# A decoder layer in split float32: GpSimd makes the low parts of the weights, and the bias table DMAs go by SyncE's queue

## Chip, cores and metric

One core of one Trainium2 chip runs the kernel in one launch. The metric is the time on the device in microseconds (us). The kernel before takes 1284.85 us, the median of three runs (1284.72 to 1285.17).

## What is computed

One layer of a hybrid decoder with 512 tokens and a model width of 1024, all float32: a half-step gated feed-forward block (width 2816), a mixer of two attention branches whose outputs are gated and summed, and a second half-step feed-forward block. The weights are read once from HBM.

```python
x = x + 0.5 * swiglu(rms_norm(x, ffn1_norm), ffn1_w_gate, ffn1_w_up, ffn1_w_down)
h = rms_norm(x, mix_norm)
c_q, c_kv, k_rope, q_d, k_d, v_d, g_a, g_b = split(h @ w_in)
y_a = causal_latent_attention(c_q, c_kv, k_rope; w_uq, w_ukv) @ w_br_mla      # 8 heads
y_b = dilated_attention(q_d, k_d, v_d; T5 bias of rel_bias) @ w_br_dil        # 3 groups of 8 heads
x = x + (sigmoid(g_a + b_a) * y_a + sigmoid(g_b + b_b) * y_b) @ w_out
x = x + 0.5 * swiglu(rms_norm(x, ffn2_norm), ffn2_w_gate, ffn2_w_up, ffn2_w_down)
y = rms_norm(x, norm_final)

def swiglu(h, w_gate, w_up, w_down):
    return (silu(h @ w_gate) * (h @ w_up)) @ w_down
```

## The kernel before

Activations lie transposed in SBUF, features on the 128 partitions and the 512 tokens along the row. A weight product is done in three matmuls for each 128x128 tile: a float32 operand is the sum of a high part, rounded to the fast format, and a low part, and TensorE computes high by high, high by low and low by high (`multiply`, lines 365 to 377; the up products have the same three in line 540).

All weights come as one stream of 222 pieces of up to eight tiles (128x1024, 512 KB), numbered through the whole kernel: `up1` 44, `down1` 24, `latent` 6, `mla` 16, `dil` 48, `merge` 8, `out` 8, `up2` 44, `down2` 24. The down products' pieces have 8, 7 and 7 tiles, the latent up-projections ("lora") 5, and two of every twelve dilated pieces 4. For each piece:

- SyncE issues its load into one of four raw buffers (`load`, line 345). It waits until the low part of the piece four back is made.
- ScalarE makes the high part `w_hi` in one of two split buffers (`split_hi`, line 351). It waits for the load and until the piece two back is multiplied.
- VectorE makes the low part `w_lo = raw - w_hi` (`split_lo`, line 359) and counts it in `lo_ready`.
- TensorE waits for `lo_ready` and multiplies, and counts the piece in `piece_done`.

Each engine's order is written out by hand, so every split stands at a fixed place between the other operations of ScalarE and VectorE. The places that matter here:

- Start: x comes in eight chunks, and pieces 0 to 3 among them (lines 412 to 424). Up product (`up_turn`): two pieces make a gate and an up chunk; VectorE scales the gate (L1255), ScalarE takes the silu, VectorE scales and multiplies (L1259, L1261), ScalarE rounds the hidden chunk (L914), VectorE makes its low part (L1266). Before the first piece 3, TensorE spreads the norm over the tokens (L507) behind its wait for the low part of piece 3.
- Second turn of the first up product: VectorE also computes the rotation angles (L1196 to L1223) and the rows of the T5 bias (`bias_rows`, L1229, `rows_ready`). GpSimd then stores 16 copies of these rows to HBM (`skew`, L470), and after the last lora product reads them back as bias tables with 24 DMAs (L480), since their SBUF is shared with the latents.
- Down product (`down_turn`): after the third part of a chunk VectorE adds to x (L1284), ScalarE rounds the new activation (L875) and squares it (L885), VectorE makes the activation's low part (L1170) and adds the square (L1182). The second part's high part stands behind these on ScalarE.
- Latent attention (`attention`): for a head, VectorE takes the maxima of the scores (L1445), ScalarE the exponentials (L1022), VectorE normalises (L1458); in between it takes the next head's key, value (L1437, L1438) and query (L1420 to L1433).
- Merge: VectorE multiplies gate and branch (L1683, L1687) and adds (L1691), ScalarE rounds (L1133), VectorE makes the low part (L1694). The next high part stands behind L1133. Output product: VectorE adds to x (L1703), then ScalarE and VectorE go on as in the down product.

Before the change GpSimd does only small DMAs and, at the very end, two multiplications of the output (L486).

## Time and profile before

| what | value |
|---|---|
| median of three runs | 1284.85 us |
| the profiled execution | 1285.54 us |
| its span, first to last instruction | 1283.7 us |
| granted TensorE clock, mean | 0.999 |
| chain that ended last, shares | TensorE 94%, VectorE 2%, DMA 1%, issue 1%, ScalarE 1% |
| HBM | 92 GB/s over the span, 118 MB |

The profile is one execution, so its time stands beside the median and not for it. Its times are microseconds from the span's start. Its engines are PE (TensorE's matmuls), PEld (its weight loads), DVE (VectorE), ACT (ScalarE), POOL (GpSimd) and SP (SyncE); L361 is line 361 of the kernel before. TensorE is at work all the time and heads the chain, so a time is best read by where two matmul starts lie further apart than usual, and by how long before a piece's first matmul its low part was there. Matmuls are pipelined, so a duration of 0.39 us says little; the distance of starts does.

### The profile page before, as it was taken

The numbers are of one execution on the slowest core, as the hardware profiler recorded it, in microseconds if no ns is written. First come the engines' busy times: TensorE is split into PE (matmuls) and PEld (weight loads), VectorE is DVE, ScalarE is ACT, GpSimd is POOL, SyncE is SP. The second block draws the span as 40 slices with busy tenths as digits, with TensorE's granted clock in tenths as the row PEclk, the third lists the DMA queues.
The fourth block names the chain that finished last, engine by engine and source line by source line (L and its number), as shares of the span: only waits on it lengthen the run. The fifth ranks groups of instructions, "written<-read, shape, count | busy, mean of one in ns | idle before, by whom it ended". The sixth has DMA issues, their size and how long they took to land.

```text
span 1283.7 us, 16607 instructions
## 1 busy us (share of the span) xinstructions
PE 1270.7 (99%) x5998; PEld 1031.0 (80%) x5998; DVE 669.6 (52%) x984; ACT 442.9 (35%) x763; POOL 18.8 (1%) x36
## 2 busy tenths in 40 slices
PE   9999999999999999999999999999999999999997
PEld 6788888888888777787878878788888888888886
DVE  5744444433336777575655747676644444443323
ACT  5333322322233445343343424423433322332221
POOL 0000000000000000300000000000000000000000
PEclk9999999999999999999999999999999999999999
DMA  6342223333322221522222121223222223233321
GB/s 213 99 112 98 98 98 98 90 91 94 102 92 71 64 69 66 131 67 82 81 73 93 65 92 56 83 97 99 99 98 98 98 98 98 95 86 96 93 89 65
DMA packets 36003, 118.38 MB, mean 92 GB/s; under 512 B 4680, under 2 KB 4680, under 8 KB 35968
## 3 DMA queue, kind: packets, MB, share of 16 engines
q1 hardware_dynamic: 34416, 114.83, 27.6%
q0 software_dynamic: 1264, 3.06, 1.4%
q8 instruction: 20, 0.33, 0.1%
q14 instruction: 15, 0.12, 0.0%
q10 hardware_dynamic: 288, 0.03, 0.0%
HBM read 115.36 MB, written 2.55 MB: 92 GB/s over the span
## 4 chain that ended last, share of the span: by engine, by line
PE 94%; DVE 2%; DMA 1%; issue 1%; ACT 1%; SPq 0%; DVEq 0%; ACTq 0%
PE bank L540 36%; PE bank L374 17%; PE bank L376 17%; PE bank L375 17%; PE bank L723 1%; PE bank L746 1%; PE bank L643 1%; PE bank L670 1%; DMA x<-in_x_t 1%; DVE mla_stats L1445 1%; PE bank L763 1%; PE bank L659 1%; PE bank L759 1%; ACT w_hi L356 0%; PE bank L732 0%
## 5 line engine op out<-in xcount | busy, mean ns | idle before, releaser
L361 DVE TENSOR_TENSOR w_lo<-raw,w_hi 128x1024 fp32r<-128x1024 f32 (+2 forms) x221 | 258.8, 1171 | 228.8 <-ACT w_hi L356 226.7
L356 ACT ACTIVATE w_hi<-raw 128x1024 fp32r<-128x1024 f32 (+2 forms) x221 | 224.3, 1015 | 429.7 <-PE bank L540 228.3
L540 PE MATMUL bank<-act_hi,w_hi 128*128 128x512 f32 x704 | 217.8, 391 | 1.6 <-DVE act_lo L1170 0.8
L540 PE MATMUL bank<-act_hi,w_lo 128*128 128x512 f32 x704 | 216.9, 389 | 0.0
L540 PE MATMUL bank<-act_lo,w_hi 128*128 128x512 f32 x704 | 216.8, 389 | 0.0
L374 PE MATMUL bank<-act_hi,w_hi 128*128 128x512 f32 x528 | 212.0, 401 | 2.0 <-DVE w_lo L361 1.2
L376 PE MATMUL bank<-act_hi,w_lo 128*128 128x512 f32 x528 | 206.2, 391 | 0.0
L375 PE MATMUL bank<-act_lo,w_hi 128*128 128x512 f32 x528 | 205.8, 390 | 0.0
L540 PEld LDWEIGHTS bank<-act_hi,w_hi 128*128 128x128 f32 x704 | 131.6, 188 | 31.7 <-DVE w_lo L361 2.6
L540 PEld LDWEIGHTS bank<-act_hi,w_lo 128*128 128x128 f32 x704 | 132.1, 188 | 27.7
L540 PEld LDWEIGHTS bank<-act_lo,w_hi 128*128 128x128 f32 x704 | 132.1, 188 | 27.4
L375 PE MATMUL bank<-hid_lo,w_hi 128*128 128x512 f32 x352 | 136.9, 389 | 0.0
L374 PE MATMUL bank<-hid_hi,w_hi 128*128 128x512 f32 x352 | 136.9, 389 | 0.0
L376 PE MATMUL bank<-hid_hi,w_lo 128*128 128x512 f32 x352 | 136.9, 389 | 0.0
L374 PEld LDWEIGHTS bank<-act_hi,w_hi 128*128 128x128 f32 x528 | 99.1, 188 | 27.2 <-issue 6.0
L376 PEld LDWEIGHTS bank<-act_hi,w_lo 128*128 128x128 f32 x528 | 99.1, 188 | 21.5
L375 PEld LDWEIGHTS bank<-act_lo,w_hi 128*128 128x128 f32 x528 | 99.3, 188 | 18.7
L1255 DVE TENSOR_TENSOR work<-bank,rstd 128x512 f32<-128x512 f32 x44 | 30.4, 691 | 122.9 <-PE bank L540 122.8
L374 PEld LDWEIGHTS bank<-hid_hi,w_hi 128*128 128x128 f32 x352 | 66.1, 188 | 13.8
L375 PEld LDWEIGHTS bank<-hid_lo,w_hi 128*128 128x128 f32 x352 | 66.1, 188 | 13.8
L376 PEld LDWEIGHTS bank<-hid_hi,w_lo 128*128 128x128 f32 x352 | 66.1, 188 | 13.5
L914 ACT ACTIVATE hid_hi<-work 128x512 f32 (+1 forms) x44 | 27.8, 632 | 94.4 <-DVE work L1261 94.4
(177 smaller groups left out, 1052.5 us busy)
## 6 DMA issues: line engine op xcount, KB each, us to landing
raw<-in_ffn_up SPq DMA_DIRECT2D x87, 512.0 KB, 3.3
raw<-in_w_dil SPq DMA_DIRECT2D x40, 512.0 KB, 3.3
raw<-in_ffn_down SPq DMA_DIRECT2D x32, 448.0 KB, 3.3
raw<-in_ffn_down SPq DMA_DIRECT2D x16, 512.0 KB, 3.5
raw<-in_w_mla_gates SPq DMA_DIRECT2D x8, 512.0 KB, 3.3
raw<-in_w_branches SPq DMA_DIRECT2D x8, 512.0 KB, 3.2
raw<-in_w_out SPq DMA_DIRECT2D x8, 512.0 KB, 3.3
raw<-in_w_latent SPq DMA_DIRECT2D x6, 512.0 KB, 3.2
```

The source lines that it names most:

```text
L356: nc.scalar.activation(w_hi[:, s % SPLIT, 0:tiles * P], raw[:, s % RAW, 0:tiles * P], ACT.Copy).then_inc(hi_ready, 1)
L361: nc.vector.tensor_tensor(w_lo[:, s % SPLIT, 0:tiles * P], raw[:, s % RAW, 0:tiles * P], w_hi[:, s % SPLIT, 0:tiles * P].bitcast(F32), ALU ...
L374: nc.tensor.matmul(out, a, hi(k), start=first, stop=False)
L375: nc.tensor.matmul(out, a, lo(k), start=False, stop=False)
L376: last = nc.tensor.matmul(out, b, hi(k), start=False, stop=end)
L540: last = nc.tensor.matmul(out, w[:, s % SPLIT, tile * P:(tile + 1) * P], moving[:, row, :], start=row == 0 and w is w_hi and moving is act_hi,
L643: nc.tensor.matmul(out, mla_q[0:QK_DIM, h % 2, b * P:(b + 1) * P], mla_k[0:QK_DIM, h % 2, 0:(b + 1) * P], start=True, stop=False, skip_gro ...
L659: last = nc.tensor.transpose(bank[5 + unit % 2][:, at:at + P], mla_p[:, row * P:(row + 1) * P], ident)
L670: last = nc.tensor.matmul(bank[7][V_DIM * e:V_DIM * (e + 1), key * P:SEQ], mla_v[:, e, key, :], probs_t[:, e, at:at + width], start=key == ...
L723: last = nc.tensor.matmul(out, dil_q[rows, g, b * P:(b + 1) * P], dil_k[rows, g, keys], start=True, stop=True, skip_group_check=True)
L914: nc.scalar.activation(hid_hi[:, bass.ds(2 * i + 2 * turn + j, 1), :], work[:, 3:4, :], ACT.Copy).then_inc(hid_rounded, 1)
L1255: nc.vector.tensor_tensor(work[:, 0, :], bank[c % UP_BANKS][:, :], rstd[:, :], ALU.mult).then_inc(chunk_taken, 1)
```

## The change

- All low parts from piece 3 on are made by GpSimd, in the order of the stream, behind its five small DMAs at the start. VectorE keeps those of pieces 0 to 2, and all other splits leave its order. The shapes, buffers and waits of `split_lo` stay as they are.
- GpSimd no longer issues the store of the skew rows and the 24 bias table DMAs; SyncE does. The store stands in SyncE's order behind the loads of the up product's turns 1 and 2 (pieces 4 to 11) and ahead of piece 12's, with its wait for `rows_ready`. The bias DMAs stand behind the loads of the first three dilated pieces and wait for `skew_stored` and the last lora product.
- The load of piece 2 is issued ahead of the last chunk of x.
- High parts move on ScalarE: piece 4's, from the second half of the first turn to the end of the first half's splits; and in the last latent head, the second dilated piece's, from behind the exponentials to ahead of them, with the third's staying behind them.

```diff
-        def split_lo(dve, s, d, tiles):
-            dve.wait_ge(hi_ready, s + d + 1)
-            nc.vector.tensor_tensor(w_lo[:, s % SPLIT, 0:tiles * P], raw[:, s % RAW, 0:tiles * P],
+        def split_lo(engine, operations, s, d, tiles):
+            engine.wait_ge(hi_ready, s + d + 1)
+            operations.tensor_tensor(w_lo[:, s % SPLIT, 0:tiles * P], raw[:, s % RAW, 0:tiles * P],
                                     w_hi[:, s % SPLIT, 0:tiles * P].bitcast(F32),
                                     ALU.subtract).then_inc(lo_ready, 1)
...
+            def store_skew():
+                sp.wait_ge(rows_ready, 1)
+                row = t5_row[:, :].rearrange("h (a n) -> h a n", a=1).to_broadcast([GROUP_HEADS, COPIES, T5_END])
+                sp.dma_start(skew.rearrange("c h n -> h c n"), row).then_inc(skew_stored, 16)
+
+            def load_biases():
+                sp.wait_ge(skew_stored, 16)
+                sp.wait_ge(piece_done, PIECES["mla"] + 2 * MLA_HEADS - 1)
+                for g, width in enumerate((2 * P, P, P)):
+                    for first in range(0, P, COPIES):
...
+                        sp.dma_start(table, source).then_inc(bias_loaded[g], 16)
...
             def load_ffn(f):
                 load_up_turn(f, 0, 0)
-                with sp.Fori(0, KF // 2 - 1) as i:
-                    load_up_turn(f, 1, i)
+                early = 0 if f else 2
+                for turn in range(early):
+                    load_up_turn(f, 1 + turn, 0)
+                if f == 0:
+                    store_skew()
+                with sp.Fori(0, KF // 2 - 1 - early) as i:
+                    load_up_turn(f, 1 + early, i)
                 load_down(f)
...
             for k in range(HALF, KM):
                 sp.wait_ge(x_loaded[k - HALF + 1], 16)
+                if k == KM - 1:
+                    load(sp, 2, 0, ffn[0][0][2], TILES)
                 load_x(k)
...
+            def load_dilated(i, first=False):
                 for q in range(10):
                     load(sp, PIECES["dil"] + q, 12 * i, w_dil[bass.ds(i, 1), q].rearrange("a p n -> p (a n)"), TILES)
+                    if first and q == 2:
+                        load_biases()
...
+            def split(s, d, tiles):
+                split_lo(pool, nc.gpsimd, s, d, tiles)
...
+            pool.wait_ge(lo_ready, 3)
+            split_up(0, 3)
+            split_down(0)
+            for q in range(6):
+                split(PIECES["latent"] + q, 0, TILES)
...
+            split_up(1, 0)
+            split_down(1)
...
-                    else:
+                    elif not (first and f == 0):
                         split_hi(act, s + 2, 4 * i, TILES)
                     split_hi(act, s + 3, 4 * i, DOWN_PARTS[1][1] - DOWN_PARTS[1][0] if last and j else TILES)
+                    if first and f == 0 and j == 0:
+                        split_hi(act, s + 4, 0, TILES)
...
                 take_values(h, i)
-                exponentials(h, i)
-                split_hi(act, s + 2, d, following[0])
                 if h == MLA_HEADS - 1:
+                    split_hi(act, s + 2, d, following[0])
+                    exponentials(h, i)
                     split_hi(act, s + 3, d, following[1])
+                else:
+                    exponentials(h, i)
+                    split_hi(act, s + 2, d, following[0])
```

On VectorE all other calls of `split_lo` are taken out (in `up_turn`, `down_turn`, the latent projections, `attention`, `dilated_pair`, merge and output).

## Rows read from the trace of the kernel before

**Rows 1.** The page's first part: busy us (share of the span) x instructions.
```profile
PE 1270.7 (99%) x5998; PEld 1031.0 (80%) x5998; DVE 669.6 (52%) x984; ACT 442.9 (35%) x763; POOL 18.8 (1%) x36
```
**Rows 2.** Timeline of TensorE, latent attention: start us, us, instruction, [idle before].
```profile
423.81 0.39 PE L376 MATMUL bank<-lat_hi,w_lo 128*128 128x512 f32 x1
424.60 0.49 PE L374 MATMUL bank<-act_hi,w_hi 128*128 128x512 f32 x1 [0.40 <-DVE mla_vt L1438]
...
437.70 0.39 PE L376 MATMUL bank<-lat_hi,w_lo 128*128 128x512 f32 x1
438.22 0.49 PE L374 MATMUL bank<-act_hi,w_hi 128*128 128x512 f32 x1
...
527.43 0.39 PE L376 MATMUL bank<-act_hi,w_lo 128*128 128x512 f32 x1
528.99 0.47 PE L374 MATMUL bank<-act_hi,w_hi 128*128 128x512 f32 x1 [1.18 <-DVE w_lo L361]
```
**Rows 3.** Timelines of ScalarE and TensorE, first up product, piece 12.
```profile
72.03 1.06 ACT L356 ACTIVATE w_hi<-raw 128x1024 fp32r<-128x1024 f32 x1 [1.02 <-PE bank L540]
...
77.27 0.61 PE L540 MATMUL bank<-act_hi,w_hi 128*128 128x512 f32 x2
```
**Rows 4.** Timelines of ScalarE and TensorE, third piece of the merge.
```profile
830.88 1.05 ACT L356 ACTIVATE w_hi<-raw 128x1024 fp32r<-128x1024 f32 x1
...
833.92 0.43 PE L374 MATMUL bank<-act_hi,w_hi 128*128 128x512 f32 x1
```
**Rows 5.** Timelines of ScalarE and TensorE, fourth piece of the output product.
```profile
880.06 1.05 ACT L356 ACTIVATE w_hi<-raw 128x1024 fp32r<-128x1024 f32 x1
...
883.30 0.39 PE L374 MATMUL bank<-merged_hi,w_hi 128*128 128x512 f32 x1
```
**Rows 6.** Timelines of ScalarE, VectorE and TensorE, second part of a down chunk.
```profile
268.38 0.94 ACT L356 ACTIVATE w_hi<-raw 128x896 fp32r<-128x896 f32 x1
...
268.74 0.68 DVE L1182 TENSOR_TENSOR sumsq<-sumsq,square 128x512 f32<-128x512 f32 x1
269.35 1.09 DVE L361 TENSOR_TENSOR w_lo<-raw,w_hi 128x896 fp32r<-128x896 f32 x1
...
271.75 0.39 PE L374 MATMUL bank<-hid_hi,w_hi 128*128 128x512 f32 x1
```
**Rows 7.** Timelines of GpSimd and ScalarE at the end of the kernel.
```profile
1276.81 2.49 POOL L486 TENSOR_TENSOR x<-work,rstd 128x512 f32<-128x512 f32 x2 [751.05 <-ACT rstd L1146]
...
1276.08 0.58 ACT L1146 COPY rstd<-bank 128x512 f32<-128x512 f32 x1 [2.49 <-PE bank L507]
```
**Rows 8.** Timelines of TensorE and VectorE, second latent head: scores and maxima.
```profile
433.42 0.63 PE L645 MATMUL bank<-mask_causal,mask_ident 128*128 128x128 f32 x1
...
433.74 1.23 DVE L361 TENSOR_TENSOR w_lo<-raw,w_hi 128x1024 fp32r<-128x1024 f32 x1 [1.86 <-ACT w_hi L356]
434.89 1.68 DVE L1445 TENSOR_REDUCE mla_stats<-bank 128x1 f32<-128x128 f32 x4
```
**Rows 9.** Timelines of ScalarE and TensorE at the start, pieces 2 to 4.
```profile
16.48 1.06 ACT L356 ACTIVATE w_hi<-raw 128x1024 fp32r<-128x1024 f32 x1 [1.03 <-DMA raw<-in_ffn_up]
...
23.49 1.05 ACT L356 ACTIVATE w_hi<-raw 128x1024 fp32r<-128x1024 f32 x1
...
25.95 1.12 PE L507 MATMUL bank<-const,token_rstd 128*128 128x128 f32 x8
...
33.57 0.74 PE L540 MATMUL bank<-act_hi,w_hi 128*128 128x512 f32 x2 [0.29 <-DVE w_lo L361]
```
**Rows 10.** VectorE's bias rows; DMA issues (KB, us to landing) and SyncE's timeline.
```profile
61.93 1.21 DVE L1229 TENSOR_TENSOR t_row<-bank,t_mask 8x383 f32<-8x383 f32 x3
...
skew<-t_row POOLq DMA_DIRECT2D x1, 446.5 KB, 10.6
...
64.44 15.85 SPq L349 DMA_DIRECT2D raw<-in_ffn_up  x4
raw<-in_ffn_up SPq DMA_DIRECT2D x1, 512.0 KB, 10.8
```

More of the change, by code:

```diff
@@ new lines, in split_up, with split_down @@
+            def split_up(f, first):
+                for q in range(first, 4):
+                    split(PIECES[f"up{f + 1}"] + q, 0, TILES)
+                with pool.Fori(0, KF // 2 - 1) as i:
+                    for q in range(4):
+                        split(PIECES[f"up{f + 1}"] + 4 + q, 4 * i, TILES)
+            def split_down(f):
+                with pool.Fori(0, 2) as i:
+                    for q in range(12):
+                        a, b = DOWN_PARTS[q % 3]
+                        split(PIECES[f"down{f + 1}"] + q, 12 * i, b - a)
@@ L483, in _ @@
+            for phase in ("merge", "out"):
+                with pool.Fori(0, KM // 4) as i:
+                    for q in range(4):
+                        split(PIECES[phase] + q, 4 * i, TILES)
+            split_up(1, 0)
+            split_down(1)
             for k in range(POOL_CHUNKS):
```

73 lines of the change are left out of this document (23 added, 50 removed).

## The prediction

> **What bounds the kernel now.** I read the page's busy line first: TensorE is at work nearly all of the span, VectorE half of it, GpSimd hardly [rows 1]. So taking the low parts off VectorE (1.23 us for a full piece [rows 8]) shortens nothing by itself. It can only remove the places where TensorE waits, and it can make new ones. I then read TensorE's start times. Matmuls of 512 columns start every 0.227 us, so a piece of 24 takes 5.44 us; where two starts lie further apart, TensorE waited. Past the first 34 us such places are few and all lie in the latent attention: 424.60 after 423.81 (0.56 over the pace), 438.22 after 437.70 (0.29; two more heads show the same), and 528.99 after 527.43 (1.34, ended by a w_lo) [rows 2]. Sum 0.56 + 3 x 0.29 + 1.34 = 2.77 us. That, and parts of the start, is all that the change can win: about 0.2% of the span.
>
> Next I read how late each weight piece is ready. Its high part (ScalarE) can start only when the piece two back is done, because there are two split buffers; the low part follows; TensorE needs it when the piece in between ends. So the question for each stage is the time from the end of w_hi to the start of the piece. In the up products it is 77.27 - 73.09 = 4.18 us [rows 3]. It is shortest where ScalarE first finishes an activation chain: merge 833.92 - 831.93 = 1.99 us [rows 4], output product 883.30 - 881.11 = 2.19 us [rows 5], second down part 271.75 - 269.32 = 2.43 us [rows 6]. VectorE's 1.23 us fits in all of them.
>
> **What GpSimd's low part costs.** The trace shows GpSimd's TENSOR_TENSOR at 128x512 only: 1.26 us, two in 2.49, started 0.15 us after ScalarE's end (1276.66 to 1276.81) [rows 7]. On VectorE 896 columns take 1.09 and 1024 take 1.23 us [rows 6, 8]: 1.09 ns a column, so about 0.67 at 512. Lower bound for GpSimd at 1024: a column costs it no less than VectorE, 1.26 + 512 x 1.09 ns = 1.82 us; upper bound: twice 1.26 = 2.52. VectorE's ratio of 1024 to 512 is 1.83, which would make 2.30. I take 2.38, between that and the upper end; for 896 columns 2.1. The sum's own range goes by 2.30 to 2.52, and 1.82 is rival A. To that come the 0.15 us before it and some 0.05 us to TensorE: 2.58 us behind the end of w_hi, where VectorE needs about 1.3.
>
> **Part by part.** (1) Merge: 2.58 - 1.99 = 0.59 us too late. Each piece waits for the end of the piece two back, so a shortfall is paid once in two pieces. Eight pieces of this kind (six of merge, two of output): 4 x 0.59 = 2.4 us. (2) Output product: 2.58 - 2.19 = 0.39; eight pieces (the last two are the first of the second up stage): 4 x 0.39 = 1.6 us. With 2.30 and 2.52 the two together are 3.3 and 5.1 (4 x 0.51 + 4 x 0.31, 4 x 0.73 + 4 x 0.53). I take 3.9 (2.4 + 1.6, rounded). (3) Down product, second part: 2.1 + 0.2 = 2.3 against 2.43: fits by 0.1 us; 0 to 0.8 us, taken 0.1. The other pieces of the down products, the up products and the dilated attention leave over three microseconds each and hide it. (4) Start, piece 3: w_hi ends 24.54; TensorE today goes on at 25.95 without a wait, because the wait for the low part stands ahead of the spread matmuls [rows 9]. With GpSimd it is ready at 24.54 + 2.58 = 27.12: +1.17 us. Piece 4, whose high part is now made in the first half turn, no longer waits, which gives back the 0.29 us at 33.57 [rows 9] and little more. Net +0.8 (0.3 to 1.2). The third raw piece is loaded ahead of the last x chunk. ScalarE waited 1.03 us for it [rows 9], but has x's rounding and a square ahead of it in its queue, and x now lands later: -0.4 to +0.4, taken 0. (5) Latent attention: the low part at 433.74 stood ahead of the maxima on VectorE, which began at 434.89 though the scores ended at 434.05 [rows 8]. Without it maxima, key and value come 0.75 us earlier, more than the 0.29 that TensorE waits; at 424.60 it is the same order with the same 1.23 us ahead of the maxima, taken as enough for 0.56. At the last head the high part moved ahead of the exponentials runs while ScalarE waits for the maxima, and its low part no longer waits for the normalising (1.06 + 2.58 us in all, begun some 5 us ahead of 527.65). All 2.77 us go; what is late next is TensorE itself.
>
> (6) The DMAs. On SyncE the 24 bias DMAs stand between the loads of the third and the fourth dilated piece and wait for the last lora product. Three pieces are ahead in the raw buffers, that is 16 us of products (3 x 5.44), so the fourth's load is late only if an issue takes SyncE well over half a microsecond, and even then its high part is not the next that ScalarE must deliver: 0. The store of the skew rows is the one that matters. It now stands ahead of the load of piece 12, behind a wait for the rows that VectorE ends at 63.14 [rows 10]. This DMA takes 10.6 us to land, and the 512 KB load issued at 64.44, a microsecond after it, took 10.8 and landed at 75.24 [rows 10]; it was for piece 14 and had time. Today piece 12's load is issued before the store. Afterwards it is the one behind it. Its high part starts at 72.03 and TensorE takes the piece at 77.27 [rows 3], with (4) at about 78.0. Landing is 12.1 us after the rows (75.24 - 63.14), or 11.7 with SyncE's shorter issue. The rows come between 63.0 (VectorE without low parts, everything 0.7 later) and 66.8 (two of its operations held up by GpSimd for up to 2 us each); I take 65.0. So landing 76.8 (74.7 to 78.5), TensorE's start landing + 0.1 + 1.06 + 2.58 = 80.5, a wait of 2.5 us, once (0.5 to 4.3). The next loads follow within little more than a microsecond each and are not late.
>
> The Trainium skill bears on this: by "DMA: Bandwidth & Descriptors", section "Why a DMA increments its semaphore by 16 and not by 1", a DMA from either kind of queue runs on the largest number of engines up to 16 that divides its slowest dimension, here the 8 rows, and each engine takes its ring in order. By that rule moving the store to SyncE does not speed it up, and the loads behind it wait it out; the 10.6 and 10.8 us agree. If it ran on all 16 engines instead, this wait would all but vanish.
>
> **Sum.** 3.9 + 0.1 + 0.8 - 2.77 + 2.5 = +4.5 us. The profiled execution took 1285.54 us, so 1290.1 there; the median of the runs is 0.7 lower, so 1289.4 us. With all lower ends 3.3 + 0.3 - 2.8 + 0.5 - 0.4 = +0.9, 1285.7; with all upper ones 5.1 + 0.8 + 1.2 - 2.4 + 4.3 + 0.4 = +9.4, 1294.3.
>
> **Rivals.** A: faster. GpSimd's operation is short enough for merge and output, at its lower bound of 1.82 us (2.02 behind w_hi against 1.99 and 2.19), and the skew store is out of the way; then only the 2.77 us and the start remain: 1284.85 - 2.8 + 0.3 = 1282.3. For it speaks that spans of GpSimd are rough and its two operations may overlap; against it, that 1.82 is under 1.5 times its 512-column time. B: about the same. The skew store is spread or the rows are early (0.5 us), and GpSimd takes 2.2 us (2.9 for merge and output): 2.9 + 0.8 - 2.8 + 0.5 = +1.4, 1286.3. C: slower by much. GpSimd's and VectorE's reads of SBUF hold each other up. Before shows no low part of GpSimd beside a VectorE operation with two SBUF inputs, so the price is bounded: nothing, or one 0.7 us operation in front of each low part. The latter matters in the down products, where the square sum is at work just as w_hi ends: (0.7 - 0.1) x 15 = 9 us, and in merge and output 8 x 0.7 = 5.6: 1289.4 + 14.6 = 1304. Against it: in merge and output VectorE is done with those operations before w_hi ends, and in the down product the sum ends within 0.1 us of it, so most of the price needs VectorE's operations to come later than today. D: the win in the latent attention is lost, because normalising VectorE operations on SBUF are held for the 1.5 us of a lora low part and the scores come late; 7 heads x 0.3 = 2 us more than forecast, 1291.5, inside the range.
>
> The Trainium skill has the rule behind C: "SBUF — State Buffer", section "Who interferes with whom", says that a VectorE instruction with two SBUF inputs and a GpSimd instruction that reads SBUF block each other for a whole instruction, whoever starts first. No row here shows it. In the up products it would hold VectorE some 1.7 us at each half turn, and TensorE would not notice.
>
> **Chances.** Forecast 0.50 and D 0.09, B 0.23, C 0.10, A 0.08. The likeliest case's own range is 1285.7 to 1294.3; with half of C and part of A left out the range is 1284.0 to 1296.5. About 0.2% (2.6 us) is what a measurement of this kernel can tell from no change, so "same" is 1282.3 to 1287.4: all of B and the low end of the forecast, 0.26; slower 0.66; faster 0.08.
>
> **What would show it.** Right: GpSimd's TENSOR_TENSOR of 128x1024 at 2.2 to 2.5 us; TensorE starting late in every second merge and output piece by 0.4 to 0.7 us; one wait of 0.5 to 4 us at piece 12 that ends with a load landing after 74.7; no waits left at the latent heads and before the second dilated piece; piece 3 about a microsecond later. Wrong: a low part under 2 or over 3 us; the piece 12 load landing by 73; waits in the down or up products; VectorE's score chain late.

## The result and the profile after

The changed kernel takes 1296.28 us (median of four, 1294.35 to 1296.88), the kernel before 1284.78 us beside it: ratio 1.0086, 95% interval 1.0074 to 1.0099, so 11.5 us slower. The profiled execution took 1294.35 us (span 1292.7) against 1285.54 (span 1283.7): 8.8 us. The rest lies in how the executions spread: the three without a profile took 2 us more (1296.24 to 1296.88 us, mean granted clock 0.996 to 0.997, where the profiled one has 0.999). Experiments 1 and 7 bear on these 2 us. One execution of experiment 6 (latent_only) took 3217.88 us at a full granted clock and is left out of its ratio.

The page of the changed kernel: the busy line, the chain's shares by engine, and two groups of its fifth part.

```profile
PE 1274.7 (99%) x5998; PEld 1030.0 (80%) x5998; DVE 529.4 (41%) x765; ACT 440.1 (34%) x763; POOL 510.0 (39%) x230
...
PE 53%; issue 30%; POOL 14%; DMA 1%; DVE 1%; POOLq 0%; ACT 0%; SPq 0%; DVEq 0%; ACTq 0%
...
L361 POOL TENSOR_TENSOR w_lo<-raw,w_hi 128x1024 fp32r<-128x1024 f32 (+1 forms) x219 | 504.5, 2304 | 750.9 <-ACT w_hi L356 750.9
...
L1307 DVE TENSOR_TENSOR work<-work,rstd 128x512 f32<-128x512 f32 x44 | 101.7, 2312 | 42.0 <-ACT work L963 42.0
```

The chain is of little help here: it puts 14% on GpSimd, while TensorE waits for low parts for some 6 us in all (next view). Against [rows 1] VectorE has 219 operations fewer, but only 140 us less work, where the low parts alone were some 256. The last row is the reason for most of that: the multiplication by rstd in the up products (line 1259 of the kernel before) took 684 ns in the mean and now takes 2312.

Which waits of TensorE are GpSimd's (view of waits, TensorE: us in total, times, longest):

```profile
PE bank L590 <- POOL w_lo L361: 3.7, 2, 2.8
...
PE bank L374 <- POOL w_lo L361: 1.3, 4, 0.4
PE bank L557 <- POOL w_lo L361: 1.0, 1, 1.0
```

L590 are the up products (L540 before): two waits, at pieces 10 and 12. L557 is the spreading of the norm ahead of piece 3, L374 the merge. These waits come to 6 us, and the kernel is 8.8 us behind. So the whole is better read from where the changed kernel falls behind the one before. These are TensorE's starts of the first matmul of a piece, taken from the two timelines:

| up to | before | after | behind by | step |
|---|---|---|---|---|
| piece 4 | 33.57 | 34.89 | 1.32 | +1.3 |
| piece 11 | 71.83 | 74.36 | 2.53 | +1.2 |
| piece 13 | 82.71 | 88.33 | 5.62 | +3.1 |
| second latent-attention piece | 411.84 | 417.58 | 5.74 | +0.1 |
| third dilated piece | 538.04 | 541.40 | 3.36 | -2.4 |
| last dilated piece | 816.86 | 821.09 | 4.23 | +0.9 |
| last merge piece | 861.31 | 867.78 | 6.47 | +2.2 |
| second piece of the second up stage | 916.40 | 925.16 | 8.76 | +2.3 |

From there to the end 0.05 us is added.

The piece 12 chain, which answers [rows 3] and [rows 10] (timelines of VectorE, SyncE, ScalarE and TensorE):

```profile
66.48 1.20 DVE L1284 TENSOR_TENSOR t_row<-bank,t_mask 8x383 f32<-8x383 f32 x3
...
67.71 0.34 SPq L406 DMA_DIRECT2D skew<-t_row  x1
68.45 8.70 SPq L349 DMA_DIRECT2D raw<-in_ffn_up  x4
...
79.20 1.06 ACT L356 ACTIVATE w_hi<-raw 128x1024 fp32r<-128x1024 f32 x1 [5.76 <-DMA raw<-in_ffn_up]
...
82.74 0.72 PE L590 MATMUL bank<-act_hi,w_hi 128*128 128x512 f32 x2 [2.78 <-POOL w_lo L361]
```

The rows are ready at 67.68, the store goes out at once, the load of piece 12 behind it, and ScalarE, free since 73.4, waits for that load until 79.20. At its usual pace TensorE would begin piece 12 at 79.80 (74.36 + 5.44); it begins at 82.74.

Merge and output product, which answer [rows 4] and [rows 5] (timelines of ScalarE, GpSimd and TensorE):

```profile
835.15 1.05 ACT L356 ACTIVATE w_hi<-raw 128x1024 fp32r<-128x1024 f32 x1
...
836.28 2.48 POOL L361 TENSOR_TENSOR w_lo<-raw,w_hi 128x1024 fp32r<-128x1024 f32 x1 [3.52 <-ACT w_hi L356]
...
838.89 0.49 PE L374 MATMUL bank<-act_hi,w_hi 128*128 128x512 f32 x1 [0.27 <-POOL w_lo L361]
...
882.61 2.39 POOL L361 TENSOR_TENSOR w_lo<-raw,w_hi 128x1024 fp32r<-128x1024 f32 x1 [3.42 <-ACT w_hi L356]
...
884.60 0.39 PE L376 MATMUL bank<-merged_hi,w_lo 128*128 128x512 f32 x1
885.06 0.50 PE L374 MATMUL bank<-merged_hi,w_hi 128*128 128x512 f32 x1
885.40 0.40 PE L375 MATMUL bank<-merged_lo,w_hi 128*128 128x512 f32 x1
```

From the second merge piece to the first of the second up stage each piece begins 0.05 to 0.24 us after its low part. The last three rows show what such a late start costs: 0.46 us from the product before in place of 0.227, and 0.34 to the next one.

The latent attention, which answers [rows 2] (timeline of TensorE): the pairs that stood 0.79 and 1.56 us apart now keep the pace.

```profile
429.40 0.39 PE L376 MATMUL bank<-lat_hi,w_lo 128*128 128x512 f32 x1
429.63 0.48 PE L374 MATMUL bank<-act_hi,w_hi 128*128 128x512 f32 x1
...
532.21 0.39 PE L376 MATMUL bank<-act_hi,w_lo 128*128 128x512 f32 x1
532.44 0.39 PE L374 MATMUL bank<-act_hi,w_hi 128*128 128x512 f32 x1
```

And what was not forecast: VectorE's operations that start while GpSimd works on a low part (timelines of GpSimd, VectorE, ScalarE and TensorE; the second turn of the first up stage, and the last latent head but one).

```profile
58.12 2.39 POOL L361 TENSOR_TENSOR w_lo<-raw,w_hi 128x1024 fp32r<-128x1024 f32 x1 [2.87 <-ACT w_hi L356]
58.20 2.86 DVE L1251 SCALAR_TENSOR_TENSOR rope<-turns,rope 64x512 f32<-64x512 f32 x1
61.10 0.69 DVE L1305 TENSOR_TENSOR work<-bank,rstd 128x512 f32<-128x512 f32 x1
...
64.89 1.06 ACT L356 ACTIVATE w_hi<-raw 128x1024 fp32r<-128x1024 f32 x1 [0.22 <-issue]
...
68.75 0.74 PE L590 MATMUL bank<-act_hi,w_hi 128*128 128x512 f32 x2 [0.92 <-POOL w_lo L361]
...
518.09 2.39 POOL L361 TENSOR_TENSOR w_lo<-raw,w_hi 128x1024 fp32r<-128x1024 f32 x1 [5.77 <-ACT w_hi L356]
...
518.11 2.66 DVE L1497 TENSOR_SCALAR mla_p<-mla_p,mla_stats 128x512 f32<-128x512 f32 x1
```

A rotation step of 0.69 us (56.76 to 57.45 for one without a low part beside it) started 0.08 us after a low part had begun and ended at 61.06, 0.55 us after that low part (60.51): it waited until GpSimd was done and then did its own work. Behind it the gate waits, then the silu, then the hidden chunk on ScalarE, and behind that the high part of piece 10 (64.89). The last row is an operation of 0.48 us with a single tensor input (and one number per partition), held in the same way.

### The profile page after: what moved, and what is told of

It is laid out like the page before. It is cut to its first block, busy times and chain, and to the rows that moved or that the text cites. A ratio compares the mean times of both kernels' runs of the same rounds, so it can differ in the third digit from the quotient of the medians.

```text
span 1292.7 us, 16764 instructions
## 1 busy us (share of the span) xinstructions
PE 1274.7 (99%) x5998; PEld 1030.0 (80%) x5998; DVE 529.4 (41%) x765; ACT 440.1 (34%) x763; POOL 510.0 (39%) x230
## 4 chain that ended last, share of the span: by engine, by line
PE 53%; issue 30%; POOL 14%; DMA 1%; DVE 1%; POOLq 0%; ACT 0%; SPq 0%; DVEq 0%; ACTq 0%
PE bank L590 32%; POOL w_lo L361 14%; PE bank L374 7%; PE bank L376 7%; PE bank L375 7%; DMA x<-in_x_t 1%; PE bank L549 0%; DVE x L1748 0%; DVE pair_sum L1371 0%; POOLq L360 0%; ACT w_hi L356 0%; PE bank L904 0%; PE bank L557 0%; DVE pair_sum L1366 0%; ACT first_squares L993 0%
## 5 line engine op out<-in xcount | busy, mean ns | idle before, releaser
L361 POOL TENSOR_TENSOR w_lo<-raw,w_hi 128x1024 fp32r<-128x1024 f32 (+1 forms) x219 | 504.5, 2304 | 750.9 <-ACT w_hi L356 750.9
L590 PE MATMUL bank<-act_hi,w_hi 128*128 128x512 f32 x704 | 218.3, 391 | 5.2 <-POOL w_lo L361 3.7
L590 PE MATMUL bank<-act_hi,w_lo 128*128 128x512 f32 x704 | 216.9, 389 | 0.0
L590 PE MATMUL bank<-act_lo,w_hi 128*128 128x512 f32 x704 | 216.8, 389 | 0.0
L374 PE MATMUL bank<-act_hi,w_hi 128*128 128x512 f32 x528 | 211.8, 401 | 1.0 <-POOL w_lo L361 1.0
L590 PEld LDWEIGHTS bank<-act_hi,w_hi 128*128 128x128 f32 x704 | 131.3, 188 | 36.4 <-POOL w_lo L361 4.5
L590 PEld LDWEIGHTS bank<-act_hi,w_lo 128*128 128x128 f32 x704 | 132.2, 188 | 27.6
L590 PEld LDWEIGHTS bank<-act_lo,w_hi 128*128 128x128 f32 x704 | 132.2, 188 | 27.5
L374 PE MATMUL bank<-hid_hi,w_hi 128*128 128x512 f32 x352 | 137.0, 389 | 0.0
L374 PEld LDWEIGHTS bank<-act_hi,w_hi 128*128 128x128 f32 x528 | 99.1, 188 | 25.8 <-issue 5.6
L1307 DVE TENSOR_TENSOR work<-work,rstd 128x512 f32<-128x512 f32 x44 | 101.7, 2312 | 42.0 <-ACT work L963 42.0
L1328 DVE SCALAR_TENSOR_TENSOR x<-bank,x 128x512 f32<-128x512 f32 x16 | 11.1, 691 | 191.2 <-PE bank L376 191.2
L374 PEld LDWEIGHTS bank<-hid_hi,w_hi 128*128 128x128 f32 x352 | 66.1, 188 | 14.3
```

The costliest lines, as they stand in the source:

```text
L361: operations.tensor_tensor(w_lo[:, s % SPLIT, 0:tiles * P], raw[:, s % RAW, 0:tiles * P], w_hi[:, s % SPLIT, 0:tiles * P].bitcast(F32), AL ...
L374: nc.tensor.matmul(out, a, hi(k), start=first, stop=False)
L590: last = nc.tensor.matmul(out, w[:, s % SPLIT, tile * P:(tile + 1) * P], moving[:, row, :], start=row == 0 and w is w_hi and moving is act_hi,
L1307: nc.vector.tensor_tensor(work[:, 2, :], work[:, 1, :], rstd[:, :], ALU.mult).then_inc(own, one())
L1328: nc.vector.scalar_tensor_tensor(out=x[:, chunk, :], in0=bank[c % UP_BANKS][:, :].rearrange("p (a n) -> p a n", a=1), scalar=0.5, in1=x[:, ...
```

## The experiments

The theory after the first reading: four costs, each with its own place (the store ahead of a load; GpSimd's length at piece 3; its length in merge and output; VectorE held behind GpSimd in the second turn and the two attentions), against a true gain in the latent attention. They should add up to the 8.8 us. The rivals stand with each experiment. Each edit is against the changed kernel unless it says otherwise.

**1. The store, one turn later.**

```diff
-                early = 0 if f else 2
+                early = 0 if f else 3
```

> The changed kernel with the skew store one turn (four loads) later on SyncE, behind the load of piece 15; nothing else. In the changed kernel's trace the store is issued at 67.71 us, as soon as VectorE has the rows, the load of piece 12 at 68.45 behind it, and TensorE waits 2.94 us for piece 12. Theory: this order alone makes that wait. The load of piece 12 then goes out at about 61 us, TensorE takes pieces 10 to 13 without a gap, and the loads behind the store have some 10 us to spare: 3.0 us less than the changed kernel, 1291.3 us for the profiled execution (1294.35). Rival: the loads behind the store are held in the queue (two of their issues took 4.77 and 2.43 us) and the wait only moves to pieces 16 to 19: within 1 us of the changed kernel. Beside it, the timed executions of the changed kernel were 2 us longer than its profiled one, at a granted clock of 0.996 against 0.999. If the wait at piece 12 is what costs them that, they come to 0.999 here and the median is within 0.7 us of the profiled execution; if not, they stay 2 us above it.

Measured: 1292.75 us (four executions, 1291.77 to 1293.28, clock 0.998 to 0.999), 1292.72 profiled, ratio 1.0059 (1.0043 to 1.0076). The store goes out at 72.88 and the wait at piece 12 is gone:

```profile
80.44 0.62 PE L590 MATMUL bank<-act_hi,w_lo 128*128 128x512 f32 x2
80.90 0.39 PE L590 MATMUL bank<-act_hi,w_hi 128*128 128x512 f32 x1
```

From piece 11 to piece 13 it gains 3.09 us on the changed kernel, and it loses nothing at pieces 16 to 19: the theory. The profiled execution is only 1.6 us shorter because this one began 1.1 us later (piece 2 at 20.42 and not 19.34), which differs from run to run (experiment 7). The median is 3.5 us lower, and the timed executions (clock 0.998 to 0.999) now lie around the profiled one.

This run also shows how many DMA engines the store uses. From 76.10 to 79.30 us no load is under way, and all 46 packets that move in this stretch (0.16 MB) are the store's. The columns are the stretch and its length, the busy time of TensorE (instructions), its weight loads, VectorE, ScalarE and GpSimd, the granted clock, the DMA share and GB/s:

```profile
76.10:79.30 3.20, 3.20 (x15) 2.63 (x14) 0.00 (x0) 0.62 (x1) 2.39 (x1) 1.00 0.47 51
```

The 16 DMA engines are busy for 0.47 of the time together: half of them carry the whole store, eight, as many as the table has rows.

**2. The low parts of the first up stage back on VectorE.**

```diff
-            pool.wait_ge(lo_ready, 3)
-            split_up(0, 3)
+            pool.wait_ge(lo_ready, PIECES["down1"])
...
+                            split_lo(dve, nc.vector, s + 3, 0, TILES)
...
+                    elif f == 0 and not (last and j):
+                        split_lo(dve, nc.vector, s + 2, 4 * i, TILES)
...
+                    if f == 0 and not (first and j == 0) and not (last and j):
+                        split_lo(dve, nc.vector, s + 3, 4 * i, TILES)
```

> The changed kernel with the low parts of the first up stage (pieces 3 to 43) back on VectorE; the rest stays on GpSimd, the store stays ahead of the load of piece 12. Theory: GpSimd's longer low part costs 1.2 us at piece 3, and VectorE's operations held by it cost 1.1 us at piece 10 and make the rows late (67.68 us against 63.13 before), which is most of the wait at piece 12. Then all three go or shrink: rows near 63.5, landing of piece 12 near 75, its wait under 1 us, in all 4.5 to 5.3 us less than the changed kernel: 1289.0 to 1289.9 us for the profiled execution. Rival: the wait at piece 12 is the store's own length and hangs little on the rows; then only 1.2 + 1.2 us come back: 1292.0. Nothing of the stages behind may move by more than 0.3 us.

Measured: 1289.34 us (six, 1288.73 to 1289.79), 1289.32 profiled, ratio 1.0034 (1.0021 to 1.0047). Against the changed kernel it gains 1.20 us at piece 3, 1.08 at piece 10 and 2.94 at piece 12, after a start that was 0.95 us later. The timelines of VectorE, SyncE and TensorE:

```profile
63.06 1.20 DVE L1283 TENSOR_TENSOR t_row<-bank,t_mask 8x383 f32<-8x383 f32 x3
...
64.29 0.34 SPq L406 DMA_DIRECT2D skew<-t_row  x1
...
78.39 0.39 PE L589 MATMUL bank<-act_hi,w_hi 128*128 128x512 f32 x1
```

With the store still ahead of the load of piece 12, the wait is not small but nothing: the rows come 3.4 us sooner, and VectorE's shorter low part does the rest. So the wait needs both the order and GpSimd in this stage. The rival (1292.0 us) falls. That VectorE's being held makes the rows late is left to experiment 3.

**3. One SBUF input in place of two.**

```diff
-                    nc.vector.tensor_tensor(work[:, 2, :], work[:, 1, :], rstd[:, :], ALU.mult).then_inc(own, one())
+                    nc.vector.tensor_tensor(work[:, 2, :], work[:, 1, :], (bank[7] if f == 0 else rstd)[:, :], ALU.mult).then_inc(own, one())
```

> The changed kernel, with the second input of VectorE's work<-work,rstd read from PSUM in the first up stage (bank 7 holds the same values there) and from SBUF as before in the second. Theory (two SBUF inputs make the operation wait out GpSimd's low part): in the first stage it takes 0.69 us again against 2.31, in the second it stays at 2.31; the activations of pieces 6 to 9 come 1.7 us earlier, the wait of 1.1 us at piece 10 goes, the rows come near 64.5 us where they came at 67.7, and the wait at piece 12 shrinks from 2.9 to about 1: in all 2.5 to 3.2 us less, 1291.2 to 1291.9 us for the profiled execution. Rival (VectorE waits for something else, such as the semaphore, the queue or SBUF as a whole): the operation stays at 2.3 us in both stages and the time at 1294.3.

Measured: 1291.13 us (four, 1290.55 to 1291.63), 1291.18 profiled, ratio 1.005 (1.0033 to 1.0066). Its groups of VectorE with the shapes kept apart, second stage and first stage, and ScalarE's timeline at piece 10:

```profile
L1307 DVE TENSOR_TENSOR work<-work,rstd 128x512 f32<-128x512 f32 x22 | 52.6, 2390 | 21.6 <-ACT work L963 21.6
L1307 DVE TENSOR_TENSOR work<-work,bank 128x512 f32<-128x512 f32 x22 | 15.1, 688 | 19.9 <-ACT work L963 19.9
...
63.35 1.06 ACT L356 ACTIVATE w_hi<-raw 128x1024 fp32r<-128x1024 f32 x1 [1.64 <-PE bank L590]
```

This is the cleanest of the comparisons. The same line in the same kernel takes 688 ns where its second input lies in PSUM and 2390 where it lies in SBUF, behind the same low parts. The high part of piece 10 again waits only for TensorE, the wait there is gone (1.08 us), the rows come at 64.72, and the wait at piece 12 shrinks by 2.58 us. By the steps one changed operand gives back 3.8 us (1.08 + 0.17 + 2.58), more than the 2.5 to 3.2 expected, although TensorE never waits for that operation itself. The profiled execution shows 3.2 of them, as it began 0.9 us later (piece 2 at 20.27). The rival falls.

**4. Merge and output product back on VectorE.**

```diff
-            for phase in ("merge", "out"):
-                with pool.Fori(0, KM // 4) as i:
-                    for q in range(4):
-                        split(PIECES[phase] + q, 4 * i, TILES)
-            split_up(1, 0)
+            split(PIECES["merge"], 0, TILES)
+            pool.wait_ge(lo_ready, PIECES["up2"] + 1)
+            split_up(1, 1)
...
+                    split_lo(dve, nc.vector, s + 1, 4 * i, TILES)
```

(the last line once in the merge and once in the output loop)

> The changed kernel with the low parts of merge pieces 1 to 7, of the output product and of the first piece of the second up stage back on VectorE. Theory: from piece 47 of the dilated attention to piece 1 of the second up stage the changed kernel falls behind by 8.76 - 4.22 = 4.5 us, all of it because a low part on GpSimd takes 2.39 us where VectorE took 1.23 and ScalarE's high part comes late. It comes back whole: 1289.8 us for the profiled execution, products of 5.44 us again. Rival: part of it is the 24 products' own stretching (5.51 to 5.58 us a piece, 16 pieces) by GpSimd's traffic elsewhere; then about 1.5 us stay: 1291.3.

Measured: 1289.50 us profiled; median 1291.95 (1289.50 to 1292.83), ratio 1.0056 (1.004 to 1.0073). From merge piece 1 to the second piece of the second up stage it gains 4.5 us (0.28 us ahead of the changed kernel at the end of the dilated attention, 4.82 after), step for step where the changed kernel lost them, and the rival (1291.3 us profiled) falls. In the timeline of TensorE the third merge piece follows without a wait:

```profile
837.64 0.39 PE L376 MATMUL bank<-act_hi,w_lo 128*128 128x512 f32 x1
837.87 0.43 PE L374 MATMUL bank<-act_hi,w_hi 128*128 128x512 f32 x1
```

The wait at piece 12 is still in this kernel, and so are the longer timed executions (1291.58 to 1292.83 at 0.996 to 0.997, the profiled one at 0.998).

**5. The dilated attention back on VectorE.**

```diff
-            with pool.Fori(0, PAIRS) as i:
-                for q in range(12):
-                    split(PIECES["dil"] + q, 12 * i, TILES if q < 10 else HALF)
+            for q in range(3):
+                split(PIECES["dil"] + q, 0, TILES)
+            pool.wait_ge(lo_ready, PIECES["merge"] + 1)
...
+                    if q > 1 or not first:
+                        split_lo(dve, nc.vector, s + q + 1, d, HALF if q in (9, 10) else TILES)
```

> The changed kernel with the low parts of the dilated attention from its fourth piece to the first merge piece back on VectorE. From the third dilated piece to the first of merge the changed kernel falls behind by 4.23 - 3.36 = 0.9 us, a little at each pair's last gate. Theory: VectorE's dil_p<-dil_p,weight (two SBUF inputs) is held there by GpSimd's low parts (0.96 us in the mean against 0.68), and the turned probabilities come late; it all comes back: 0.9 us less than the changed kernel up to the merge stage, and nothing elsewhere. Rival: the steps are the longer low part itself; that cannot be told from the total, but then the four late places would show TensorE released by a low part in the changed kernel.

Measured: 1292.37 us profiled; the timed ones spread over 5.5 us (median 1294.61, ratio 1.0082, 1.0065 to 1.0099), so the trace has to decide. It gains 0.08, 0.39, 0.14 and 0.16 us at the first half of the last gate of the four pairs, 0.8 us in all, and nothing between: as expected. In the changed kernel none of these four places is released by a low part (each is there at least 3.4 us early). Ahead of them TensorE turns values and probabilities that VectorE makes, and of these dil_p<-dil_p,weight takes 0.955 us in the mean at 128x512 (0.683 before). So GpSimd's length is not the cause, and VectorE held by GpSimd is what is left and fits; that was not tried by itself here, nor which of the held operations it is.

**6. The gain by itself.** Three kernels made from the kernel before. In the first (latent_only) GpSimd makes pieces 2 to 15 of the latent attention and the first three dilated ones, the last head's high part moves, and the bias DMAs go by SyncE; the store stays where it was. In the second (latent_mixed) the first dilated piece's low part is VectorE's again. The third (hi_moved) has the moved high part alone.

```diff
+            pool.wait_ge(lo_ready, s + 2)
+            with pool.Fori(0, 3) as i:
+                for h in range(2):
+                    split(s + 2 + 2 * h, 4 * i, LORA_TILES)
+                    split(s + 3 + 2 * h, 4 * i, TILES)
+            split(s + 14, 0, LORA_TILES)
+            split(s + 15, 0, TILES)
+            for q in range(3):
+                split(PIECES["dil"] + q, 0, TILES)
```

latent_mixed against latent_only:

```diff
-            for q in range(3):
+            pool.wait_ge(lo_ready, PIECES["dil"] + 1)
+            for q in (1, 2):
                 split(PIECES["dil"] + q, 0, TILES)
...
+                    if h == MLA_HEADS - 2:
+                        dve.wait_ge(lo_ready, PIECES["dil"])
+                        split_lo(dve, PIECES["dil"], 0, TILES)
```

hi_moved, and the same in the other two:

```diff
-                exponentials(h, i)
-                split_hi(act, s + 2, d, following[0])
                 if h == MLA_HEADS - 1:
+                    split_hi(act, s + 2, d, following[0])
+                    exponentials(h, i)
                     split_hi(act, s + 3, d, following[1])
+                else:
+                    exponentials(h, i)
+                    split_hi(act, s + 2, d, following[0])
```

> The kernel before with GpSimd's low parts only where they won: pieces 2 to 15 of the latent attention and the first three of the dilated, the last head's high part ahead of the exponentials, the bias DMAs on SyncE; the skew store stays on GpSimd's queue and all other low parts on VectorE. Theory: the gains of the latent attention stand by themselves (2.8 us at five places and about 0.6 in small ones), less 0.25 and 0.8 us where normalising operations are held behind GpSimd: 2.2 us less than the kernel before, 1283.3 us against 1285.54 profiled, ratio 0.998. Rival: the gain in the changed kernel came from elsewhere (VectorE less busy in general): within 0.5 us of the kernel before.

> The kernel with GpSimd's low parts in the latent attention alone, and of these the one of the first dilated piece back on VectorE at its old place. There GpSimd's low part started just ahead of the last normalising operation, which took 2.66 us in place of 0.48, and cost 0.8 us at the first dilated piece. Theory: that 0.8 us comes back and the 1.4 us at the second dilated piece stays won: 1281.5 us profiled, 3.9 us under the kernel before, ratio 0.997. Rival: VectorE's 1.23 us at that place delays the gate or the scores by as much: no gain over 1282.3.

> The kernel before with only the last head's high part moved ahead of the exponentials on ScalarE; all low parts stay on VectorE. Theory: the low part of the second dilated piece still stands behind the normalising operations on VectorE (527.62 to 528.84 us in the kernel before), so TensorE's wait of 1.34 us there stays within 0.2 us, and the time within 0.3 us of the kernel before: the gain at that place is GpSimd's. Rival: the high part was the late one, the wait falls by about 1 us: 1284.5 us profiled.

Measured: latent_only 1283.13 us against 1284.87, ratio 0.9986 (0.9976 to 0.9996); latent_mixed 1281.72 us against 1284.76, ratio 0.9978 (0.9969 to 0.9988), 3.0 us less and the fastest of all; hi_moved 1284.87 us against 1285.02, ratio 0.9999 (0.9989 to 1.0008). The profiled executions of the first two, 1282.30 and 1281.43 us, are not to be set against the 1285.54 of the kernel before: both began some 1 us sooner (piece 2 at 17.93 and 18.04, against 18.85). In the timelines of latent_mixed VectorE's four normalising operations (x4, the first one's shape shown) take their 1.28 us again, and the second dilated piece starts without a wait (524.80 to 525.02). The last row is hi_moved, where the same piece still waits 1.18 us for its low part:

```profile
510.67 1.28 DVE L1483 TENSOR_SCALAR mla_p<-mla_p,mla_stats 128x128 f32<-128x128 f32 x4
...
524.80 0.39 PE L376 MATMUL bank<-act_hi,w_lo 128*128 128x512 f32 x1
525.02 0.39 PE L374 MATMUL bank<-act_hi,w_hi 128*128 128x512 f32 x1
```

```profile
528.31 0.47 PE L374 MATMUL bank<-act_hi,w_hi 128*128 128x512 f32 x1 [1.18 <-DVE w_lo L361]
```

Through the latent attention latent_only gains 2.3 us on the kernel before and latent_mixed 3.0; the step between them is at the first dilated piece, where the held operation was freed. Moving the high part brings nothing while the low part stands behind VectorE's normalising. latent_only and latent_mixed have the bias DMAs on SyncE too, and no piece behind them starts later for it. The high part moved in the start was not tried by itself.

**7. The start's order and the clock.** Two kernels: the third raw piece behind x's last chunk again (raw2_last), and the skew store issued twice (store_twice).

```diff
-                if k == KM - 1:
-                    load(sp, 2, 0, ffn[0][0][2], TILES)
                 load_x(k)
             sp.wait_ge(x_loaded[HALF + 1], 16)
+            load(sp, 2, 0, ffn[0][0][2], TILES)
```

```diff
+                sp.dma_start(skew_again.rearrange("c h n -> h c n"), row).then_inc(skew_stored, 16)
                 sp.dma_start(skew.rearrange("c h n -> h c n"), row).then_inc(skew_stored, 16)
```

> The changed kernel with the third raw piece loaded behind the last chunk of x again, as in the kernel before. In the four profiles with the changed order TensorE starts piece 2 at 19.25 to 20.42 us, 1.05 us after the end of piece 1; in the two with the old order at 17.93 and 18.85, 0.12 and 0.62 after it. Theory: that order costs the difference, 0.5 to 1 us, because x's last chunk lands later: profiled 1293.3 to 1293.9 us, gap ahead of piece 2 of 0.1 to 0.6. Rival: the start is spread by a microsecond from run to run whatever the order; then the gap stays 1.05 and the median within 0.5 us of the changed kernel's 1296.3.

> The changed kernel with the skew store issued twice, the first time to a second table that nobody reads. Theory (the store's many small packets lie ahead of the load of piece 12 in the same rings): its landing comes another 7 to 10 us later and TensorE's wait grows from 2.94 to 10 to 13 us, the profiled execution to 1301 to 1304 us. Rival (the 10.6 us are a latency of each such store and not the rings' work): the two run side by side, and the wait grows by under 1.5 us: 1295.5. On the clock: if TensorE's wait is what costs the timed executions 2 us more than the profiled one, the granted clock falls after a wait this long, in the profile too, and the mean of the timed executions is 0.996 or lower.

Measured: raw2_last 1294.95 us (1294.18 to 1295.68), 1295.68 profiled, ratio 1.0078 (1.0061 to 1.0095). Piece 2 starts 1.13 us earlier than in the changed kernel, and piece 3 at 28.48 against 28.52. But this does not show that the order costs nothing. VectorE had the sum of squares ready at 21.19 us (22.55 in the changed kernel), and TensorE then waited for something else, a table of constants that GpSimd loads at the start and that landed at 22.59 here, the latest of all the profiles (19.5 to 21.9 in the others). From raw2_last's view of TensorE's waits:

```profile
PE bank L548 <- DMA const<-in_tables: 1.5, 1, 1.5
```

The timed executions speak for the theory: raw2_last's median is 1.3 us under the changed kernel's, and the mean clock is as low (0.996 to 0.997 in all four) as in the changed kernel's three longer ones. That is more than the 0.5 to 1 us of the theory, and the two kernels were not timed side by side. The rival (within 0.5 us of 1296.3) fails, and what the order costs stays open, between nothing and some 1.4 us.

On the clock this profile caught what the changed kernel's did not. The windows from 84 to 90 us (columns as in experiment 1), the changed kernel's first, and then raw2_last's, with a shorter one ahead of it and its start of piece 13 behind it:

```profile
84.00:90.00 6.00, 6.00 (x28) 4.96 (x27) 1.09 (x1) 1.70 (x2) 1.84 (x2) 1.00 0.48 168
```

```profile
83.30:86.60 3.30, 3.30 (x9) 2.54 (x8) 1.74 (x2) 0.63 (x1) 2.19 (x1) 0.50 0.47 159
...
84.00:90.00 6.00, 6.00 (x23) 4.81 (x22) 1.06 (x1) 0.63 (x1) 1.49 (x1) 0.78 0.51 171
...
89.94 0.39 PE L589 MATMUL bank<-act_hi,w_hi 128*128 128x512 f32 x1
```

Both kernels wait 2.94 us for piece 12 and start it at 82.74 and 82.75. In the one the clock stays at full speed and piece 13 follows at 88.33; in the other it is at 0.50, the lower of its two levels (1.2 GHz), from 83.30 to 86.60 and back at full speed before 90, and piece 13 follows at 89.94, 1.6 us later. If the changed kernel's timed executions lost as much, that is most of the 2 us by which they exceed the profiled one. The start can be the rest: piece 3 begins at 27.67 to 29.69 us in the profiles of the six kernels that have its low part on GpSimd and the changed order of loads, at 28.52 in the changed kernel's. The kernels with this wait have executions at a mean clock of 0.996 to 0.997 (the changed kernel, merge_vector, raw2_last, one of dil_vector), those without it stay at 0.998 to 0.999 (store_later, up1_vector, rstd_psum). It isn't the only thing that does this: two of 13 executions of the kernel before, run beside dil_vector, were at 0.997 as well (1286.83 and 1287.95 us), and so was one of ten of latent_mixed (1283.46 us).

store_twice: 1306.31 us (1306.11 to 1306.98), ratio 1.0168 (1.0151 to 1.0185). Its view of TensorE's waits and its windows:

```profile
PE bank L591 <- POOL w_lo L361: 12.7, 2, 11.8
...
84.00:90.00 6.00, 0.00 (x0) 0.00 (x0) 0.00 (x0) 0.65 (x1) 0.00 (x0) 0.53 0.74 200
90.00:96.00 6.00, 3.11 (x7) 2.48 (x8) 2.77 (x3) 2.61 (x4) 5.14 (x2) 0.50 0.46 173
```

One more store delays piece 12 by 9.0 us: the load waits out each store ahead of it, and the rival (a latency that runs beside the load) falls. The packets are larger than the expectation has them. In the changed kernel's trace the six loads from 60 to 90 us have 128 each of the 1000 packets of SyncE's queue, 104 are under 512 bytes, and 128 are left for the store's 446.5 KB, 3.5 KB each. While TensorE stands still the granted clock goes to 0.5 and is still there when piece 12 begins, which then takes 7.97 us in place of 5.59: 2.4 us more. The profiled execution of 1306.98 us is 12.6 us over the changed kernel's: 9.0, 2.4, and 1.2 at the start.

## Why the prediction came out as it did

The direction and the mechanism of most terms were right, the time was not: 1289.4 us forecast, 1296.28 measured, just inside the range (1296.5), and 2 us above what the sum's own upper ends give (1294.3). That it lies inside is in part luck: the range had been widened for half of rival C, TensorE late in the down products and in merge and output, and this did not come. Waits that the sum had at nothing took that room, and so did a lower clock and the spread of the start. By its own steps, on the profiled execution, +4.5 forecast and +8.8 measured:

- **GpSimd's low part.** Taken 2.38 and 2.1 us, measured 2.40 and 2.12 in the mean (128x1024, 128x896). Rival A falls. It starts 0.08 us behind the high part and not 0.15.
- **Merge, 2.4: measured 2.5** for the eight pieces that the text counts (six of merge, two of output: 4.41 us behind at the second merge piece, 6.93 at the second output piece), and 0.2 more at the second merge piece, which it does not count. Every second one is late by 0.43 to 0.65 us, taken 0.59.
- **Output, 1.6: measured 1.8** for its eight pieces (6.93 to 8.75). The shortfall itself was 0.27 to 0.38 us in every second piece, near the 0.39 of the text, but the pieces between lose another 0.13 each: after a late start the second product is late as well, by 0.11 us (0.34 in place of 0.227). The sum had no term for it.
- **Down products, 0.1: measured 0.2** (5.63 to 5.81 over the first down product, 0.02 at the second part of each chunk from the second on; 0.05 in the second, where the shortest lead of a low part is 0.17 us). Rival C's price was set here, 9 us, and did not come: sumsq<-sumsq,square takes 687 ns in both kernels, because it ends before the low part begins.
- **Start, 0.8: measured 1.3.** Piece 3 costs 1.20 us (experiment 2), forecast 1.17. Piece 4 gives back 0.37. The rest is a later piece 2 (19.34 against 18.85). Over all profiles piece 2 starts at 17.9 to 18.9 us where the third raw piece is loaded behind x, and at 18.5 to 20.5 where it is loaded ahead of x's last chunk. The third raw piece was taken at 0; what it costs stays open (experiment 7), but the profiles and the timed executions point to more than 0.
- **Latent attention, -2.77: measured -2.4.** All five waits went (0.57, 0.28 to 0.29 three times, 1.38), and some 0.7 us of small ones with them. But 0.25 and 0.8 us came back where normalising operations are held behind GpSimd. That was rival D, at 2 us and a chance of 0.09; its mechanism was right, and the 128x384 operation is held in six of eight heads (1433 ns in the mean, 415 before), but TensorE is late for it at two places and not in seven heads.
- **Skew store, 2.5: measured 2.9, and 0.15 behind it.** The landing was right: ScalarE starts 11.5 us after the rows, taken 11.8. The rows came at 67.68, taken 65.0, and piece 12 was due 1.8 us later than taken, and the two nearly cancel. Both have in the main the same cause, VectorE held in the second turn; the later start is the rest.
- **Bias DMAs on SyncE, 0: measured 0.**
- **Not in the sum: +1.2 at piece 10 and +0.9 in the dilated attention.** These are the steps that failed: terms put at nothing. The text names the mechanism in rival C, computes the hold in the up products (1.7 us; measured 2312 - 684 = 1.6) and concludes that TensorE would not notice. In the ordinary turns TensorE does not notice. In the second turn VectorE also has the rotation, and there the hold adds up until the high part of piece 10 is late. A hold was weighed where the engine has slack in the mean, and not in the one turn where it has none. For the first stage experiment 3 shows this cause; for the dilated attention it is what is left (experiment 5).
- **Not in the sum: the clock.** A wait of 2.9 us was priced at 2.9. In three of the four executions the mean clock is lower, and the median lies 1.9 us above the profiled execution. The kernel before's profiled execution was 0.8 us above its median. 8.8 + 1.9 + 0.8 = 11.5 us. How much of the 1.9 us is the clock is not shown: after this wait it cost 1.6 us in raw2_last's profile, the one in which it was seen to fall, and the store's place (experiment 1) takes the low mean clock away; the spread of the start is in it as well.

The rule that stood behind rival C, the Trainium skill's "SBUF — State Buffer", section "Who interferes with whom", is borne out: rows at 58.20 us (two SBUF inputs) and experiment 3 show it for two inputs. The same section of the Trainium skill says that copies and tensor_scalar operations from SBUF to SBUF can take the shared ports as well, and the trace agrees: TENSOR_SCALAR on mla_p, 0.48 us, took 2.66 behind a low part, and a 32x32 COPY rose from 187 to 697 ns in the mean. The forecast drew on the half on two inputs alone, and left the normalising to rival D. That each engine takes its ring in order, as the prediction uses it, stands in the Trainium skill in "DMA: Bandwidth & Descriptors", section "Queues, rings and completion order", and the 9.0 us of experiment 7 agree: the load waits for the stores ahead of it. That a DMA runs on as many engines, up to 16, as divide its slowest dimension stands in the Trainium skill in the section "Why a DMA increments its semaphore by 16 and not by 1" of that page, and the trace agrees: with 8 rows, the store kept 0.47 of the 16 engines busy (experiment 1).

## What to carry to other kernels

Work moved from VectorE to GpSimd is not wholly off VectorE. In this kernel the VectorE operations that read two tensors from SBUF, or copy or scale from SBUF to SBUF, waited out the low part behind which they began, so look for the turn where VectorE is fullest and not at its mean. A gain that sits in one stage is had by moving the work of that stage alone: here 16 low parts on GpSimd gave 3.0 us, and 219, with the store ahead of a load, lost 11.5. A store like the one of the skew rows, which took 9 us on half of the DMA engines, goes behind the loads that are next due, not ahead of one, even where its data is ready sooner.

## What the runs showed of the hardware

- GpSimd's subtraction of two float32 tensors takes 1.56 us at 640 columns, 2.12 at 896 and 2.40 at 1024, about twice VectorE's 1.09 and 1.23 at the last two. The 1.26 us at 512 columns [rows 7] are a multiplication; the eight subtractions of 512 columns took 1.32 to 2.08, 1.73 in the mean, most of them held by VectorE.
- VectorE and GpSimd wait for each other in both directions: a low part of 1024 columns that began while a VectorE operation of the kinds above ran took 2.48 to 2.87 us and not 2.39.
- An operation with one SBUF input and one from PSUM is not held: work<-work,bank took 688 ns in the mean behind the low parts (experiment 3). Neither is a reduction of a tensor in SBUF: stats<-dil_p took 686 ns in both kernels, and all 16 of them began during a low part.
- After TensorE had stood still for 2.8 us (its view of waits; 2.9 us behind its pace) the granted clock was 0.78 over 84 to 90 us in one execution and 1.00 in another with the same wait; in a wait of 11.8 us it fell to 0.5 before the work came back. What decides in the first case stays open.
- A store from SyncE of 446.5 KB out of 8 rows runs on half of the 16 DMA engines, and a second one holds the loads behind it for another 9.0 us.
